# Reordering VectorE and ScalarE work around the block products of a scan and of two attention openings

## The chip, the cores and the metric

The kernel runs on one core of one Trainium2 chip. The metric is the device time of one execution in microseconds (us); lower is better.

## What is computed

Six stages follow each other on one sequence of 256 tokens with 1024 channels, all in float32: convolution mixers, a mixture of 32 experts, stick-breaking attention, a second mixture of experts, a layer with a state-space scan and three groups of dilated attention (called SSD below), and a layer of block attention with 16 heads in two groups of 8 (called MOBA below). Only the last two are touched. Cut to what matters:

```python
# SSD layer; 16 scan heads, then 3 groups of 8 attention heads of 64 channels
proj = rms_norm(x) @ w_in                      # z, x|B|C, dt, q, k, v, gate
xbc  = silu(causal_conv4(xbc)); dt = softplus(dt + dt_bias); a = dt * A
cs   = cumsum(a)                               # one running sum per head
m_h  = (C_g @ B_g.T) * exp(cs_t - cs_s)        # s <= t, per head h
y_h  = m_h @ (x_h * dt_h) + d_skip * x_h
y    = rms_norm(y * silu(z)) * ssd_norm_w
q, k = rope(rms_norm(q)), rope(rms_norm(k))    # per head
o_g  = softmax(q_g @ k_g.T / 8 + mask_g) @ v_g # for each group g of 8 heads
x    = x + concat(y, weighted_sum(o_g) * silu(gate)) @ w_out
# MOBA layer; with 256 tokens there is one block, so it is causal attention
q, k, v, g = split(rms_norm(x) @ w_in)
x = x + (softmax(rope(q) @ rope(k).T / 8 + causal) @ v * silu(g)) @ w_out
```

## The kernel before

**Tiles.** The 256 tokens are two tiles of 128. Weights come as chunks of 2 MB (1024 inputs by 512 outputs) through a ring of slots in SBUF; in the last two stages a ring of three slots is in use and SyncE issues a chunk's load when its slot is free.

**Seven products for a chunk.** A projection to q, k or v of one attention group is one chunk, computed with seven block products in place of eight (a Strassen-like scheme): `seven(g, n)`, n from 0 to 6, each four matmuls of 128x256 (line 1303), which the trace records as x8. Around them stand
- `w_sums(upto)` on VectorE (line 2616): differences of weight quarters, four for a chunk, numbered on through the chunks, "up to" a count; product 1, 2, 4 and 6 each need one more of them;
- `keep(g, n)` on ScalarE (line 1851): three copies of a product's result from PSUM to SBUF. Product 2 writes where product 0's result stood and waits for the first copy, product 3 waits for the second, product 5 for the third;
- `corner(g)` on VectorE (lines 2625 and 2631): additions that build one quarter of the output. Product 6 waits for the first of them;
- `front(g)` and `crossed(g)` on VectorE (lines 2637 and 2644): the remaining additions. `crossed` ends the chunk and frees its PSUM banks for the next chunk's product 0.

**The scan** (SSD) has nine steps n = 0 to 8. In step n TensorE makes two running sums (`run_sum`, line 1496), some of the 21 products of the first group's chunks q, k, v (the list `shares` says how many in each place), the sum of squares of an earlier pair of heads (`square_sums`, line 1522) and the output of the pair before (`y`, lines 1511 and 1514). VectorE makes for two heads `decay` (lines 2813 and 2815, the arguments of the exponentials), `scan` (line 2822, product with C.B), then `gated` (lines 2827 and 2832), and in between the chunk additions, `w_sums` as the table `SCAN_SUMS` says, and `mean_squares` (lines 2572 and 2575) for the norms of q and k. ScalarE makes two exponentials (line 2013), `square` (line 2007), `squared` (line 1861), `head_root` (lines 1871 and 1872) and the copies `keep`.

**An attention group** (`attention`) starts with an opening: 16 transposes of q and k on TensorE (line 696), moved to SBUF by ScalarE (line 1639) and VectorE (line 2103). Four pairs of heads follow, each with scores (lines 1372 and 1373), mask and maximum on VectorE (`masked`, lines 2661 to 2670), exponentials on ScalarE (line 1890), transposes of them (line 1384), moves to SBUF (lines 1900 and 2678), and the product with v (`mix`, lines 1400 and 1403). Between these, TensorE fills in products of the next group's chunks; the list `shares` in `attention` says how many at each place. The groups are numbered 0, 1, 2 (SSD) and 3, 4 (MOBA); `g_no(3)` is group 3. Groups 0, 1 and 3 have a next group whose chunks they project.

**GpSimd** runs `rotate`: from the head norms it scales and rotates q and then k of a group (lines 637 to 661), and the opening of that group waits for both.

Order on each engine is the order in which its part of the code is written; every engine waits for semaphores.

## Time and profile before

| | |
|---|---|
| median of 3 runs | 1681.7 us (1680.41 to 1683.4) |
| the profiled execution's own time | 1688.95 us |
| its span | 1687.0 us |
| TensorE busy | 1574.2 us, 93% of the span |
| VectorE busy | 489.2 us, 29% |
| ScalarE busy | 265.1 us, 16% |
| GpSimd busy | 76.8 us, 5% |
| granted TensorE clock, mean | 0.985 of full |

Busy time says which engine had work recorded, not what set the end. The scan runs from about 1269 to 1333 us of the span, group 0 from 1333 to 1390, group 1 to 1439; group 2 and the output of SSD follow; MOBA's first chunks end at 1571, group 3 from 1571 to 1624, group 4 after it.

### The profile page before, as it was taken

The page shows a single profiled execution, that of the slowest core. Times are in us where ns is not written, and L with a number is a line of the kernel's source. Part 1 is how long each engine was busy: PE and PEld are TensorE (multiplying, and loading weights), DVE is VectorE, ACT ScalarE, POOL GpSimd, SP SyncE. Part 2 cuts the span into 40 slices and gives each one's busy share as a digit, 9 for nine tenths or more (in the row PEclk, how much of TensorE's full clock was granted, in tenths as well). Part 3 has the DMA queues.
Part 4 walks back from the last instruction along what each step waited for, and adds up shares of the span by engine and source line. Part 5 has one row for each costly group of instructions (what it writes and reads, how often), then busy time and mean ns, then how long its engine had stood idle before and what let it go on. Part 6 is the DMA issues. An engine that isn't in the chain of part 4 may idle for free. (4 is left out here: it accounts for less than half of the span.)

```text
span 1687.0 us, 25056 instructions
## 1 busy us (share of the span) xinstructions
PE 1574.2 (93%) x10674; PEld 1045.4 (62%) x10674; DVE 489.2 (29%) x934; ACT 265.1 (16%) x659; POOL 76.8 (5%) x138
## 2 busy tenths in 40 slices
PE   9999999998998899999999989888999989999998
PEld 8855555555455666455555655555887668648774
DVE  4941000000000313520000000004337786356542
ACT  1020000000000112210000000001222323311331
POOL 0000000000000000000000000000000342003020
PEclk9999999999999899999999999998999899999999
DMA  9679999999999832699999999997333123243320
GB/s 388 274 305 385 426 427 429 427 428 428 427 428 426 368 118 106 248 419 409 428 428 427 427 428 428 428 428 298 112 142 145 50 106 145 100 148 113 139 100 25
DMA packets 38520, 502.52 MB, mean 298 GB/s; under 512 B 4273, under 2 KB 4529, under 8 KB 6065
## 3 DMA queue, kind: packets, MB, share of 16 engines
q1 hardware_dynamic: 37872, 499.40, 71.9%
q0 software_dynamic: 576, 2.10, 0.3%
q8 instruction: 53, 0.87, 0.2%
q14 instruction: 19, 0.15, 0.0%
HBM read 500.43 MB, written 1.05 MB: 297 GB/s over the span
## 5 line engine op out<-in xcount | busy, mean ns | idle before, releaser
L854 PE MATMUL ps<-x_tok,tables_sb 128*128 128x256 f32 x1228 | 305.1, 392 | 0.0
L854 PEld LDWEIGHTS ps<-x_tok,tables_sb 128*128 128x128 f32 x1228 | 220.9, 189 | 103.5 <-issue 78.6
L877 PE MATMUL ps<-ring,arena 128*32 128x256 f32 x3968 | 238.6, 382 | 32.5 <-DMA ring<-in_expert_up 23.4
L877 PEld LDWEIGHTS ps<-ring,arena 128*32 128x32 f32 x3968 | 118.7, 109 | 141.3 <-issue 30.7
L719 PE MATMUL ps<-spare,ring 128*128 128x256 f32 x768 | 169.5, 383 | 1.3 <-DVE spare L2108 1.3
L2344 DVE TENSOR_TENSOR arena<-arena,ps 128x128 f32<-128x128 f32 x64 | 18.4, 288 | 499.3 <-ACT arena L1723 499.3
L719 PEld LDWEIGHTS ps<-spare,ring 128*128 128x128 f32 x768 | 147.2, 192 | 22.7 <-DVE spare L2108 1.6
L940 PE MATMUL ps<-ring,arena 128*32 128x512 f32 x928 | 115.1, 612 | 16.3 <-ACT arena L1718 11.3
L1303 PE MATMUL ps<-ring 128*128 128x256 f32 x480 | 114.8, 393 | 3.6 <-issue 3.6
L1303 PEld LDWEIGHTS ps<-ring 128*128 128x128 f32 x480 | 92.8, 196 | 21.9 <-issue 9.2
L751 PE MATMUL ps<-ring,arena 128*128 128x512 f32 x224 | 98.7, 596 | 2.9 <-ACT arena L1841 1.3
L1303 PE MATMUL ps<-ring,spare 128*128 128x256 f32 x360 | 88.6, 397 | 7.7 <-DVE tables_sb L2625 6.0
L1723 ACT ACTIVATE arena<-ps 128x128 f32<-128x128 f32 x64 | 17.8, 278 | 459.1 <-PE ps L877 459.1
L1303 PEld LDWEIGHTS ps<-ring,spare 128*128 128x128 f32 x360 | 69.7, 198 | 21.1 <-DVE ring L2616 6.7
L2616 DVE TENSOR_TENSOR ring<-ring 128x1024 f32<-128x1024 f32 x60 | 73.5, 1259 | 6.0 <-DMA ring<-in_stream 4.8
L751 PEld LDWEIGHTS ps<-ring,arena 128*128 128x128 f32 x224 | 41.7, 190 | 53.8 <-issue 49.1
L899 PE MATMUL ps<-arena,root_w 128*128 128x512 f32 x128 | 59.7, 607 | 14.6 <-DVE arena L2355 13.1
L2355 DVE COPY arena<-ps 128x512 f32<-128x512 f32 x16 | 11.1, 692 | 204.3 <-PE ps L940 204.3
L940 PEld LDWEIGHTS ps<-ring,arena 128*32 128x32 f32 x928 | 26.0, 110 | 69.9 <-issue 67.7
L833 PE MATMUL ps<-arena,x_tok 128*128 128x128 f32 x512 | 60.5, 276 | 0.8 <-DVE arena L2303 0.8
L833 PEld LDWEIGHTS ps<-arena,x_tok 128*128 128x128 f32 x512 | 58.6, 192 | 1.9 <-DVE arena L2303 1.1
L899 PEld LDWEIGHTS ps<-arena,root_w 128*128 128x128 f32 x128 | 22.8, 189 | 52.9 <-DVE arena L2355 27.7
(298 smaller groups left out, 1402.4 us busy)
## 6 DMA issues: line engine op xcount, KB each, us to landing
ring<-in_expert_up SPq DMA_DIRECT2D x124, 2048.0 KB, 20.9
ring<-in_stream SPq DMA_DIRECT2D x43, 2048.0 KB, 8.4
ring<-in_expert_down SPq DMA_DIRECT2D x42, 2048.0 KB, 25.1
ring<-in_expert_down SPq DMA_DIRECT2D x32, 1024.0 KB, 23.3
arena<-in_expert_up SPq DMA_DIRECT2D x4, 2048.0 KB, 11.2
arena<-in_expert_down SPq DMA_DIRECT2D x2, 2048.0 KB, 12.3
tables_sb<-in_expert_down SPq DMA_DIRECT2D x2, 2048.0 KB, 9.9
spare<-in_expert_down SPq DMA_DIRECT2D x2, 2048.0 KB, 10.3
```

Source lines behind the costliest of these rows:

```text
L719: ins = pe.matmul(o, w[:, k, m * P:(m + 1) * P], xT[:, k, :], start=(k == 0), stop=(k == KT - 1))
L751: ins = pe.matmul(bank(2 * t + n), mixT[:, 4 * c + k, t * P:(t + 1) * P], w[:, k, n * 512:(n + 1) * 512], start=(c == 0 and k == 0), stop= ...
L833: ins = pe.matmul(ps[:, b, n * P:(n + 1) * P], x[:, t, k * P:(k + 1) * P], pick[:, t].rearrange("p e s -> p (e s)"), start=(t == 0), stop= ...
L854: pe.matmul(ps[:, b, 0:TOK], ident, x[:, 0, 0:TOK], start=True, stop=True, skip_group_check=True)
L877: ins = pe.matmul(ps[q * SLOTS:(q + 1) * SLOTS, 4 + e % 2, 0:TOK] .rearrange("p (g n) -> p g n", g=2), xg[:, 4 * half + k, e * SLOTS:(e + ...
L899: return pe.matmul(bank(2 * t + n), back[:, t * P:(t + 1) * P], yg[:, n * 512:(n + 1) * 512], start=False, stop=False, skip_group_check=True)
L940: ins = pe.matmul(ps[e * SLOTS:(e + 1) * SLOTS, 6 + n, :], hidT[:, e, k * SLOTS:(k + 1) * SLOTS], v, start=(k == 0), stop=(k == 3), skip_g ...
L1303: ins = pe.matmul(o, i[:, k, :], m[:, k, :], start=(opens and k == 0), stop=(k == 3), skip_group_check=True)
L1723: act.activation(sg[:, e % 2, :], ps[:, 4 + e % 2, 0:P], ACT.Silu).then_inc(s("silu"), 1)
L2344: dve.tensor_tensor(hid[:, e % 2, :], sg[:, e % 2, :], ps[:, 4 + e % 2, P:TOK], mul)\
L2355: dve.tensor_copy(yg[:, 512:], bank(7)).then_inc(s("yg_moved"), 1)
L2616: dve.tensor_tensor(w_sum[n % W_SUMS], a_, b_, sub).then_inc(sem("w_sums"), 1)
```

## The change

Nothing is computed otherwise; instructions change places on three engines. The transposes of group 3's opening go to other PSUM banks (4, 5, 2, 3 in place of 0, 1, 2, 3), since bank 0 takes the next chunk's products.

```diff
-SCAN_SUMS = (10, 12, 12, 15, 16)
+SCAN_SUMS = (10, 12, 12, 14, 15, 15, 16)
...
         def qk_banks(n):
-            return (0, 1, 2, 3) if n == g_no(3) else (4, 5, 2, 3)
+            return 4, 5, 2, 3
...   TensorE, attention
-                shares = [3, 3 if grp != g_no(3) else 4, 3, 4, 3, 4]
+                shares = [3, 3, 3, 4, 3, 4]
...
-                elif parts and grp != g_no(3):
+                elif parts:
                     some(1)
-                elif grp != g_no(3):
+                else:
...   TensorE, scan
-                shares = [2, 2, 3, 2, 2, 3, 2, 1, 1, 1, 1, 1]
+                shares = [2, 2, 3, 2, 2, 3, 1, 1, 2, 1, 1, 1]
...   ScalarE, attention
-                if grp != g_no(3):
-                    keep(q, 1)
+                keep(q, 1)
                 exps(0)
-                if grp == g_no(3):
-                    keep(q, 1)
                 keep(q, 2)
...   ScalarE, scan
                 for n in range(SSD_HEADS // 2):
+                    c = g + 6 + n // 2
+                    if n in (0, 2, 4):
+                        keep(c, 0)
+                    elif n == 5:
+                        keep(c, 1)
                     for h in (2 * n, 2 * n + 1):
                         act.wait_ge(sem("ss_arg"), 2 * (h + 1))
                         act.activation(ss_arg[:, h % 2, :], ss_arg[:, h % 2, :], ACT.Exp)\
                             .then_inc(sem("ss_e"), 1)
-                    c = g + 6 + n // 2
-                    if n in (0, 2, 4):
-                        keep(c, 0)
+                    if n in (0, 2):
                         keep(c, 1)
+                    if n == 5:
+                        keep(c, 2)
                     if n in (2, 4):
                         squared(0, "qk"[(n - 2) // 2])
                     if n >= 1:
                         square(n - 1)
-                    if n in (0, 2, 4):
+                    if n in (0, 2):
                         keep(c, 2)
...   ScalarE, before group 3
                 keep(g + 2, 1)
+                keep(g + 2, 2)
                 head_root(n, "k")
-                keep(g + 2, 2)
...   VectorE, attention (groups 0, 1, 3)
                 masked(3)
-                w_ahead(16)
                 corner(k)
+                w_ahead(14)
                 front(k)
                 crossed(k)
...
                 front(v)
+                w_ahead(15)
                 crossed(v)
+                w_ahead(16)
...   VectorE, scan
-                        if n in (1, 3, 6):
-                            corner(g + 6 + n // 2 - n // 6)
+                        if n in (1, 3):
+                            corner(g + 6 + n // 2)
                         scan(2 * n)
                         scan(2 * n + 1)
-                    if n in (1, 3, 7):
-                        front(g + 6 + n // 2 - n // 7)
                     if n in (1, 3):
+                        front(g + 6 + n // 2)
                         crossed(g + 6 + n // 2)
                     if n >= 1:
                         gated(n - 1)
+                    if n in (3, 5):
+                        mean_squares(0, "qk"[(n - 3) // 2])
                     if n < len(SCAN_SUMS):
                         w_sums(SCAN_SUMS[n])
-                    if n in (3, 5):
-                        mean_squares(0, "qk"[(n - 3) // 2])
+                    if n == 7:
+                        corner(g + 8)
+                        front(g + 8)
                 crossed(g + 8)
...   VectorE, before group 3
                 crossed(g + 1)
-                mean_squares(n, "k")
                 w_sums(c + 14)
                 corner(g + 2)
                 w_sums(c + 16)
                 front(g + 2)
                 crossed(g + 2)
+                mean_squares(n, "k")
```

In groups 1 and 3 the counts of `w_ahead` are capped at what is left of the chunks, and nothing is left for 14, 15 and 16; there `w_ahead` does nothing at the changed places.

How the instructions stand now, at three places. In the changed kernel the same code has line numbers that differ by a few.

VectorE in group 0, at the end of `masked(3)` (last row of it first), before:

```order
L2670 TENSOR_SCALAR spare<-spare 128x2x2
L2616 TENSOR_TENSOR ring<-ring 128x1024 x3
L2625 TENSOR_TENSOR tables_sb<-tables_sb,ps 128x256
L2631 TENSOR_TENSOR arena<-tables_sb 128x256
L2637 TENSOR_TENSOR arena<-tables_sb,ps 128x256
L2644 TENSOR_TENSOR arena<-tables_sb,ps 128x2x256
```

And in the changed kernel (2672 was 2670, 2627 was 2625, 2618 was 2616):

```order
L2672 TENSOR_SCALAR spare<-spare 128x2x2
L2627 TENSOR_TENSOR tables_sb<-tables_sb,ps 128x256
L2633 TENSOR_TENSOR arena<-tables_sb 128x256
L2618 TENSOR_TENSOR ring<-ring 128x1024
L2639 TENSOR_TENSOR arena<-tables_sb,ps 128x256
L2646 TENSOR_TENSOR arena<-tables_sb,ps 128x2x256
```

Three weight differences stood ahead of `corner(k)`; now none does, one stands behind it, and the other two behind `front(v)` and `crossed(v)`.

ScalarE in steps 4 and 5 of the scan (2013 is an exponential, 1851 a copy `keep`, 1861 `squared`, 2007 `square`), before:

```order
L2013 ACTIVATE arena<-arena 128x384 x2
L1851 ACTIVATE tables_sb<-ps 128x256 x2
L1861 ACTIVATE arena<-arena 128x1024
L2007 ACTIVATE arena<-arena 128x256
L1851 ACTIVATE tables_sb<-ps 128x256
L2013 ACTIVATE arena<-arena 128x384 x2
L2007 ACTIVATE arena<-arena 128x256
```

And in the changed kernel (2015 was 2013, 2004 was 2007):

```order
L1851 ACTIVATE tables_sb<-ps 128x256
L2015 ACTIVATE arena<-arena 128x384 x2
L1861 ACTIVATE arena<-arena 128x1024
L2004 ACTIVATE arena<-arena 128x256
L1851 ACTIVATE tables_sb<-ps 128x256
L2015 ACTIVATE arena<-arena 128x384 x2
L1851 ACTIVATE tables_sb<-ps 128x256
L2004 ACTIVATE arena<-arena 128x256
```

The first copy of v's products went ahead of step 4's exponentials, the second to the start of step 5, behind step 4's `square`, the third behind step 5's exponentials.

TensorE in the opening of group 3, from the transposes on, before:

```order
L696 MATMUL ps<-tables_sb,arena 128x128 x16
L1372 MATMUL ps<-arena 128x128
L1373 MATMUL ps<-arena 128x256
L1372 MATMUL ps<-arena 128x128
L1373 MATMUL ps<-arena 128x256
L1303 MATMUL ps<-ring,spare 128x256 x4
L1303 MATMUL ps<-ring 128x256 x8
L1384 MATMUL ps<-tables_sb,spare 128x128 x6
```

And in the changed kernel:

```order
L696 MATMUL ps<-tables_sb,arena 128x128 x16
L1303 MATMUL ps<-ring,spare 128x256 x4
L1372 MATMUL ps<-arena 128x128
L1373 MATMUL ps<-arena 128x256
L1372 MATMUL ps<-arena 128x128
L1373 MATMUL ps<-arena 128x256
L1303 MATMUL ps<-ring 128x256 x12
L1384 MATMUL ps<-tables_sb,spare 128x128 x6
```

Product 0 of the next q chunk now stands between the transposes and the scores that wait for them; one product fewer follows later.

## Rows read from the trace of the kernel before

**Rows 1.** Timeline of TensorE in the scan: start, us, line, [idle before, releaser].

```profile
1272.73 3.69 PE L1303 MATMUL ps<-ring 128*128 128x256 f32 x16 [0.88 <-issue]
...
1307.95 3.75 PE L1303 MATMUL ps<-ring 128*128 128x256 f32 x8 [2.71 <-issue]
...
1326.77 0.70 PE L1522 MATMUL ps<-arena,tables_sb 128*128 128x256 f32 x2 [2.17 <-ACT arena L2007]
...
1329.02 1.12 PE L1511 MATMUL ps<-arena 128*64 128x256 f32 x4 [0.28 <-DVE arena L2822]
...
1335.11 1.09 PE L696 MATMUL ps<-tables_sb,arena 128*128 128x128 f32 x8 [0.61 <-DVEq L2861]
```

**Rows 2.** Timeline of ScalarE in step 4 of the scan.

```profile
1307.48 0.64 ACT L1851 ACTIVATE tables_sb<-ps 128x256 f32<-128x256 f32 x2
```

**Rows 3.** Timeline of VectorE in steps 3 to 7 of the scan.

```profile
1300.70 3.68 DVE L2616 TENSOR_TENSOR ring<-ring 128x1024 f32<-128x1024 f32 x3
...
1305.63 0.48 DVE L2813 SCALAR_TENSOR_TENSOR arena<-ps,tables_sb 128x256 f32<-128x256 f32 x1
...
1309.57 2.06 DVE L2616 TENSOR_TENSOR ring<-ring 128x1024 f32<-128x1024 f32 x1
1312.88 0.48 DVE L2813 SCALAR_TENSOR_TENSOR arena<-ps,tables_sb 128x256 f32<-128x256 f32 x1 [1.26 <-PE ps L1496]
...
1318.29 0.48 DVE L2827 SCALAR_TENSOR_TENSOR arena<-arena,tables_sb,ps 128x256 f32<-128x256 f32 x1 [2.63 <-PE ps L1514]
...
1321.85 0.41 DVE L2625 TENSOR_TENSOR tables_sb<-tables_sb,ps 128x256 f32<-128x256 f32 x1
...
1322.64 2.71 DVE L2822 TENSOR_TENSOR arena<-arena 128x384 f32<-128x384 f32 x2
...
1327.51 1.46 DVE L2822 TENSOR_TENSOR arena<-arena 128x384 f32<-128x384 f32 x2
```

**Rows 4.** Timeline of TensorE in group 0, around its longest idle time.

```profile
1365.08 1.89 PE L1303 MATMUL ps<-ring,spare 128*128 128x256 f32 x8
1372.03 3.65 PE L1303 MATMUL ps<-ring,spare 128*128 128x256 f32 x8 [5.07 <-DVE tables_sb L2625]
```

**Rows 5.** Timeline of VectorE in group 0, after `masked(3)`.

```profile
1367.27 4.28 DVE L2616 TENSOR_TENSOR ring<-ring 128x1024 f32<-128x1024 f32 x3
1371.48 0.41 DVE L2625 TENSOR_TENSOR tables_sb<-tables_sb,ps 128x256 f32<-128x256 f32 x1
```

**Rows 6.** Timeline of TensorE in the opening of group 3.

```profile
1571.46 1.91 PE L696 MATMUL ps<-tables_sb,arena 128*128 128x128 f32 x16
1575.32 0.50 PE L1372 MATMUL ps<-arena 64*128 64x128 f32 x4 [1.95 <-ACT arena L1639]
...
1576.18 3.18 PE L1303 MATMUL ps<-ring,spare 128*128 128x256 f32 x8
1579.16 4.16 PE L1303 MATMUL ps<-ring 128*128 128x256 f32 x16
```

**Rows 7.** Windows of 2 us: PE, PEld, DVE, ACT, POOL busy, granted clock, DMA share.

```profile
1314.00:1316.00 2.00, 2.00 (x7) 1.55 (x6) 1.66 (x4) 0.71 (x2) 1.18 (x2) 0.50 0.00 0
...
1577.00:1579.00 2.00, 2.00 (x6) 1.62 (x5) 1.93 (x5) 0.00 (x0) 0.00 (x0) 0.50 0.62 262
```

**Rows 8.** Timeline of VectorE ahead of group 3.

```profile
1546.40 1.22 DVE L2572 TENSOR_REDUCE spare<-arena 128x16 f32<-128x1024 f32 x1 [1.12 <-ACT arena L1861]
...
1559.42 0.67 DVE L2644 TENSOR_TENSOR arena<-tables_sb,ps 128x512 f32<-128x512 f32 x1
```

**Rows 9.** Timeline of GpSimd ahead of group 3: the rotations of q and of k.

```profile
1537.37 0.22 POOL L637 TENSOR_TENSOR spare<-spare 128x16 f32<-128x16 f32 x1 [102.00 <-ACT spare L1872]
...
1543.87 0.46 POOL L661 TENSOR_TENSOR arena<-arena 128x128 f32<-128x128 f32 x1
...
1558.04 1.43 POOL L661 TENSOR_TENSOR arena<-arena 128x128 f32<-128x128 f32 x1
```

**Rows 10.** Timeline of GpSimd in step 6 of the scan.

```profile
1322.41 2.53 POOL L646 TENSOR_TENSOR arena<-arena,spare 128x512 f32<-128x512 f32 x2
```

## The prediction

> **What bounds the kernel now.** I read the page first: TensorE is busy for nearly all of the span, so an edit can only pay where it waits. Then I read the list of TensorE's waits. Most are in the two mixtures of experts, which the change does not touch. In the scan and the attention groups few are longer than 0.9 us, and I looked at each in the timelines. Three lie where the change works.
>
> In the scan TensorE stands idle four times of note: 0.88, 2.71, 2.17 and 0.28 us, and 0.61 us in the opening behind it [rows 1]. The 2.71 us before 1307.95 are v's product 2. It waits for the first copy of product 0, which ScalarE makes at 1307.48 [rows 2], behind two exponentials. These wait for the decays that VectorE begins only at 1305.63, because three weight differences from 1300.70 (3.68 us) and a reduction stand ahead [rows 3].
>
> In group 0 product 6 of k waits 5.07 us for the first addition of `corner(k)` [rows 4]. That addition took 0.41 us at 1371.48, but from 1367.27 on VectorE was making three weight differences (4.28 us) [rows 5].
>
> In the opening of group 3 the scores wait 1.95 us for ScalarE to move the transposes [rows 6].
>
> After each of these the clock costs again. At 1314 to 1316 and 1577 to 1579 the granted clock is 0.50, the 1.2 GHz level in place of 2.4 [rows 7]. A product takes 1.89 us at full clock and 3.65 or 3.75 us behind the two long waits [rows 1, 4]; behind the 1.95 us it took 3.18 us and the two after it 4.16 us [rows 6]. After idle times of 0.88 us [rows 1] nothing of this is seen: the two products there took 3.69 us together.
>
> **Group 0.** `corner(k)` moves to the end of `masked(3)`, ahead of all three differences. It can start at 1367.27, since product 4 and the copies it waits for are done. So it starts 1371.48 - 1367.27 = 4.2 us earlier, and TensorE waits 5.07 - 4.2 = 0.9 us. Such a wait left the clock alone, so product 6 takes 1.85 and not 3.65 us: 1.8 us more. Together 6.0 us; if the clock falls all the same, 4.2. The three differences now stand one behind `corner(k)` and one each behind `front(v)` and `crossed(v)`. They are needed for products 2, 4 and 6 of the next group's q. The one behind `crossed(v)` (1.23 us, a third of 3.68) is ahead of VectorE's two moves of the next opening; TensorE has 1.8 us of transposes and 1.85 us of a product there, against 0.7 + 1.2 + 1.6 = 3.5 us of VectorE. It fits with nothing to spare: I charge 0.1. **Term: 5.9, bounds 4.1 and 6.0.** In groups 1 and 3 the moved differences are capped away.
>
> **Opening of group 3.** One product (1.83 us from start to start) goes into the wait of 1.95, which the moves and not the transposes set, so the scores start where they did and one product is gone from behind them: 1.8. TensorE then idles 0.1 us, and I expect no fall of the clock: the slow product gives back 3.18 - 1.89 = 1.3, the two after it 4.16 - 3.69 = 0.5. **Term: 3.6, bounds 1.8 and 3.6.** Products 2 and 3 of q need copies, and both come well before the places they now stand at, as in groups 0 and 1, which have this order already and no wait.
>
> What this could cost is `mean_squares` of k, moved from 1546.40 to behind `crossed`, which ends at 1559.42 + 0.67 = 1560.1 [rows 8]. From there: reduction and roots 1.9, and the rotation on GpSimd 1543.87 + 0.46 - 1537.37 = 7.0 us, so 1569.0, against transposes at 1571.46. The other rotation ended at 1558.04 + 1.43 = 1559.5 [rows 9], 13.1 us behind its reduction's start; that length would end at 1573.2, 1.7 us late. But it ran beside four weight differences, and after 1560.1 VectorE has nothing to do there: I take 1569.0 and no cost. The differences that lay beside it should run a little faster and bring `corner` of v earlier: 0.2 us.
>
> **The scan.** Copy 0 ahead of the exponentials takes away the 0.88 us (ScalarE was idle ahead of them). In step 3 two differences stand in place of three (-1.23). So the decays of step 4 start at 1305.63 - 0.88 - 1.23 = 1303.5, 2.1 us earlier.
>
> From there VectorE is what bounds. Before, it went from 1305.63 to the end of the last scans, 1327.51 + 1.46 = 1328.97: 23.3 us, of which 1.26 + 2.63 = 3.9 were idle, both waiting for TensorE while it ran at half clock. In step 6 `corner(v)` (1322.64 - 1321.85 = 0.8) goes behind the last scans. One difference comes in addition (1.23 us free, 2.06 as the one at 1309.57 took). So 23.3 - 3.9 - 0.8 + 1.2 or 2.1 = 19.8 or 20.7 us, and the last scans end at 1323.3 or 1324.2: 5.7 or 4.8 us earlier. `corner(v)` behind `gated(6)` (0.9 + 0.4) is covered by the last `y`, which took 1.1 us and more from 1329.02.
>
> Against this stand new waits. v's product 3 now needs copy 1, which is behind `square(3)`: decays 1.3, scans 1.2 to 2.7, `gated` 0.9 to 1.5, square 0.4, copy 0.4 from 1303.5 on, so 1307.7 to 1309.8, and TensorE is there at about 1307 (1307.95 - 2.71 - 0.88 = 1304.4, a running sum that waits for the decays, and product 2): a wait of 0.7 to 2.8 where 2.71 was. At its long end the clock falls as before, and the 3.9 us of VectorE's idle time come back. The wait of 2.17 us for `square(5)` stays, since step 6's scans meet the rotation of k again (2.71 us at 1322.64 against 1.46 at 1327.51, beside the GpSimd rows at 1322.41 [rows 10]). The difference now in step 6 makes a second wait of some 2 us ahead of the last `y`, and then v's product 6 may run at half clock (+1.8). The gain lies between 0.6 (5.7 less 3.9 and less 1.2 for locked scans) and 5.7; nearer the free end, since the lighter step 3 acts in any case. **Term: 4.3, bounds 0.6 and 5.7.**
>
> Here a rule speaks against the change. The two scans at 1322.64 took 2.71 us while GpSimd multiplied [rows 10]. The Trainium skill, page "SBUF — State Buffer", on the engine ports, says that VectorE's second port pair is shared with GpSimd as an exclusive lock: an instruction with two SBUF inputs and a GpSimd instruction do not share, one waits for the other to end. The trace agrees with it. By it the rotation of q, which now starts earlier, would catch the scans of step 4 (2.7 us, not 1.2) and the difference behind them (2.06, not 1.23), and the term would be 4.3 - 1.5 - 0.8 = 2.0, the sum 11.7.
>
> **Sum.** 5.9 + 3.6 + 0.2 + 4.3 = 14.0 us. The profiled execution took 1688.95 us (span 1687.0 and 1.95 around it), 7.25 more than the median of 1681.7; 1688.95 - 14.0 = 1674.95, and at the median's level 1681.7 - 14.0 = **1667.7 us**.
>
> **The rivals.**
> - *All three waits go (forecast), 0.60*: 1667.7; its own bounds 1681.7 - 15.5 = 1666.2 and 1681.7 - 9.9 = 1671.8 (with 2.5 or less of the scan, 4.1 in group 0).
> - *The scan gives nothing, 0.18*: product 3 waits 2.8 us in place of product 2, the clock falls, and VectorE's idle time returns. 5.9 + 3.6 + 0.2 + 0.6 = 10.3, so 1671.4. For it: the copy is behind `square(3)`, which is behind locked scans. Against it: TensorE has one product more to do before it needs the copy.
> - *Group 0's wait moves on, 0.08*: with a later weight difference the next group's q waits for one of its sums, or the 0.9 us are enough for the clock. It takes back 4: 1671.7 to 1673. Against it: product 4 of q is some 7 us behind the opening.
> - *Group 3's opening waits for the rotation, 0.05*: 1.7 us late, then the clock falls as behind 1.95 us; the term of 3.6 is gone: 1671.3.
> - *The change doesn't do what it says, 0.05*: each wait has a second cause just behind the first that no row of before shows. 1681.7, give or take 1.5.
> - *Slower, 0.04*: the clock. What spares the time must not bring it down elsewhere. In the scan it was still at 0.50 in the window from 1314 to 1316 [rows 7], 6 to 8 us behind the wait that ended at 1307.95. Half clock costs a half of its length, so against 14.0 us gained it decides from 28 us of new half clock on, and 35 us make 1685. Place: the scan's last three steps, with two waits of 2 us close together, and on into group 0. Against it: behind the waits of 2.17 and 0.28 us the eight transposes at 1335.11 took 1.09 us [rows 1], at the rate of the sixteen in 1.91 [rows 6].
>
> **How the numbers follow.** What a measurement of this kernel can tell from no change is about 0.2%, 3.4 us. Faster by more (below 1678.3): 0.60 + 0.18 + 0.08 + 0.05 = 0.91, less 0.02 for mixtures of the bad cases, 0.89. Same: 0.05 + 0.02 = 0.07. Slower: 0.04. The range reaches from the best bound less the runs' own spread of 1.5 us, 1664.5, to the worse cases with the low bounds of two terms at once, 1681.7 - 6 = 1675.7.
>
> **What would show it.** Group 0: product 6 of k begins within 1 us of product 5's end and takes 1.9 us. Group 3: a product stands between transposes and scores, idle time ahead of the scores under 0.3 us, the clock at 1.00 behind it, and the transposes not held by GpSimd. Scan: v's product 2 without a wait, one ahead of product 3 of 0.7 to 2.8 us, two of about 2 us in steps 7 and 8. The forecast is wrong if the clock is at 0.50 for over 10 us of the scan, if a wait of 1 us or more stands in group 1's start, or if the transposes of group 3 wait for the rotation.

## The result and the profile after

The changed kernel takes **1670.7 us** in the median of 4 executions (1668.54 to 1672.73), against 1682.0 (1680.41 to 1683.4) beside it. The ratio is 0.9919, interval 0.9903 to 0.9936: 13.6 us less, 10.8 to 16.3. The two medians stand 11.3 us apart, which the interval holds too. The forecast was 1667.7 us with 14.0 us gained. On a second chip the ratio was 0.991 (0.9891 to 0.9929). Single executions far above the rest, at a low granted clock, are left out of every ratio, and so is the trace of the first series of the scan's part below, which is of one (2698.5 us at 0.555).

The first lines of the page of the changed kernel:

```profile
span 1669.8 us, 25056 instructions
...
PE 1565.3 (94%) x10674; PEld 1039.7 (62%) x10674; DVE 487.1 (29%) x934; ACT 264.9 (16%) x659; POOL 73.1 (4%) x138
```

The same instructions on the same engines; TensorE is busy for 8.9 us less (the span is 17.2 shorter). The same matmuls took less time, at a mean granted clock of 0.990 for 0.985.

**Three stretches.** I measure each from one TensorE row to another. *Scan*: from the start of q's product 1 in step 1 (before: the 8 matmuls that end where the wait of 0.88 us begins, 2.77 us ahead of the row of 1272.73 [rows 1]; after: the row of 24 at 1268.53, since no wait divides them) to the second half of group 0's transposes. *Group 0*: from there to group 1's transposes. *Opening 3*: from group 3's transposes to the next ones. The rows at the ends that are not shown elsewhere, of before:

```profile
1269.96 1.89 PE L1303 MATMUL ps<-ring 128*128 128x256 f32 x8
...
1390.22 1.91 PE L696 MATMUL ps<-tables_sb,arena 128*128 128x128 f32 x16
...
1623.89 1.91 PE L696 MATMUL ps<-tables_sb,arena 128*128 128x128 f32 x16
```

and of the change:

```profile
1377.94 1.91 PE L696 MATMUL ps<-tables_sb,arena 128*128 128x128 f32 x16
...
1606.62 1.91 PE L696 MATMUL ps<-tables_sb,arena 128*128 128x128 f32 x16
```

| stretch | before | after | gained | forecast |
|---|---|---|---|---|
| scan | 65.15 | 60.21 | 4.9 | 4.3 |
| group 0 | 55.11 | 49.20 | 5.9 | 5.9 |
| opening 3, with group 3 | 52.43 | 49.00 | 3.4 | 3.6 |

The three add up to 14.3 us. The span is 17.2 shorter: 1.4 us of the rest lie ahead of the scan, and 1.6 us at the first chunks of MOBA, in a place that the change does not touch (see "A fourth place" below).

TensorE in the scan after the change, timeline:

```profile
1268.53 5.34 PE L1303 MATMUL ps<-ring 128*128 128x256 f32 x24
...
1303.93 1.99 PE L1303 MATMUL ps<-ring 128*128 128x256 f32 x8
1307.25 1.97 PE L1303 MATMUL ps<-ring 128*128 128x256 f32 x8 [1.33 <-ACT tables_sb L1851]
...
1316.99 0.70 PE L1522 MATMUL ps<-arena,tables_sb 128*128 128x256 f32 x2 [0.16 <-ACT arena L2004]
...
1321.19 0.65 PE L1511 MATMUL ps<-arena 128*64 128x256 f32 x4 [2.70 <-DVE arena L2826]
...
1322.74 3.65 PE L1303 MATMUL ps<-ring,spare 128*128 128x256 f32 x8 [0.68 <-DVE tables_sb L2627]
...
1328.74 1.09 PE L696 MATMUL ps<-tables_sb,arena 128*128 128x128 f32 x8 [0.61 <-DVEq L2867]
```

The waits of 0.88 and 2.71 us [rows 1] are gone: v's product 2 is the row of 1303.93, without idle time. Product 3 has one of 1.33 for its copy. The 2.17 us for `square(5)` have become 0.16. A new wait of 2.70 us stands ahead of the last `y`, where 0.28 was, and behind it v's product 6 takes 3.65 us. The same stretch in windows of 2 us (PE, PEld, DVE, ACT and POOL busy, then the granted clock, the DMA share and GB/s):

```profile
1322.00:1324.00 2.00, 1.32 (x5) 1.11 (x4) 1.86 (x6) 0.42 (x1) 0.58 (x1) 0.70 0.00 0
1324.00:1326.00 2.00, 2.00 (x6) 1.55 (x6) 0.31 (x1) 0.42 (x1) 0.00 (x0) 0.50 0.03 8
```

The clock of 0.50 is the level of 1.2 GHz.

VectorE in steps 3 to 8 of the same scan; L2618 is the weight difference, L2826 the two scans of a step:

```profile
1299.39 2.55 DVE L2618 TENSOR_TENSOR ring<-ring 128x1024 f32<-128x1024 f32 x2
...
1303.19 2.28 DVE L2826 TENSOR_TENSOR arena<-arena 128x384 f32<-128x384 f32 x2
...
1306.30 1.48 DVE L2618 TENSOR_TENSOR ring<-ring 128x1024 f32<-128x1024 f32 x1
...
1314.10 1.21 DVE L2826 TENSOR_TENSOR arena<-arena 128x384 f32<-128x384 f32 x2
...
1316.41 2.06 DVE L2618 TENSOR_TENSOR ring<-ring 128x1024 f32<-128x1024 f32 x1
...
1319.71 1.42 DVE L2826 TENSOR_TENSOR arena<-arena 128x384 f32<-128x384 f32 x2
```

and GpSimd beside them:

```profile
1302.69 2.36 POOL L646 TENSOR_TENSOR arena<-arena,spare 128x512 f32<-128x512 f32 x2
...
1314.81 2.58 POOL L646 TENSOR_TENSOR arena<-arena,spare 128x512 f32<-128x512 f32 x2
```

Two differences stand where three stood, and the decays follow at 1301.86. The scans of step 4 ran into the rotation of q (2.28 us), those of step 6 began ahead of the multiplications of k's (1.21), and the difference behind them ran into it (2.06).

TensorE in group 0 and in the opening of group 3, the answers to [rows 4] and [rows 6]:

```profile
1361.45 1.97 PE L1303 MATMUL ps<-ring,spare 128*128 128x256 f32 x8 [0.85 <-DVE tables_sb L2627]
...
1557.62 1.91 PE L696 MATMUL ps<-tables_sb,arena 128*128 128x128 f32 x16
1559.36 1.89 PE L1303 MATMUL ps<-ring,spare 128*128 128x256 f32 x8
1561.47 0.50 PE L1372 MATMUL ps<-arena 64*128 64x128 f32 x4 [0.21 <-ACT arena L1639]
...
1562.33 5.45 PE L1303 MATMUL ps<-ring 128*128 128x256 f32 x24
```

Product 6 of k waits 0.85 us in place of 5.07 and runs at full clock. In group 3 a product stands between transposes and scores, and the 24 matmuls behind are at full clock.

### The profile page after: what moved, and what is told of

Its sections match the earlier page's. It is cut to its first block and busy times, and to the rows that moved or that the text cites. A ratio compares the mean times of both kernels' runs of the same rounds, so it can differ in the third digit from the quotient of the medians.

```text
span 1669.8 us, 25056 instructions
## 1 busy us (share of the span) xinstructions
PE 1565.3 (94%) x10674; PEld 1039.7 (62%) x10674; DVE 487.1 (29%) x934; ACT 264.9 (16%) x659; POOL 73.1 (4%) x138
## 5 line engine op out<-in xcount | busy, mean ns | idle before, releaser
L940 PE MATMUL ps<-ring,arena 128*32 128x512 f32 x928 | 114.2, 608 | 16.9 <-ACT arena L1718 11.3
L1303 PE MATMUL ps<-ring 128*128 128x256 f32 x480 | 110.4, 383 | 1.3 <-ACT tables_sb L1851 1.3
L2618 DVE TENSOR_TENSOR ring<-ring 128x1024 f32<-128x1024 f32 x60 | 72.8, 1243 | 8.9 <-DMA ring<-in_stream 7.6
```

The source lines that it names most:

```text
L940: ins = pe.matmul(ps[e * SLOTS:(e + 1) * SLOTS, 6 + n, :], hidT[:, e, k * SLOTS:(k + 1) * SLOTS], v, start=(k == 0), stop=(k == 3), skip_g ...
L1303: ins = pe.matmul(o, i[:, k, :], m[:, k, :], start=(opens and k == 0), stop=(k == 3), skip_group_check=True)
L2618: dve.tensor_tensor(w_sum[n % W_SUMS], a_, b_, sub).then_inc(sem("w_sums"), 1)
```

## The experiments

Every kernel was timed between executions of the kernel before on the same chip. The table gives them all; "less" is the time below before by the ratio, with its interval, and the three stretches are those of its trace, measured as above.

| kernel | executions | median us | ratio (95%) | us less | scan | group 0 | opening 3 |
|---|---|---|---|---|---|---|---|
| before, again | 12 | 1684.36 | 1.0007 (0.9994, 1.002) | -1.2 | 65.18 | 55.09 | 52.44 |
| group part alone | 6 | 1675.77 | 0.9951 (0.9936, 0.9966) | 8.2 | 62.12 | 49.21 | 50.74 |
| the same, again | 12 | 1677.46 | 0.9949 (0.9931, 0.9966) | 8.6 | 65.18 | 49.21 | 50.75 |
| opening alone | 12 | 1680.97 | 0.9977 (0.9966, 0.9989) | 3.9 | 65.18 | 55.08 | 49.02 |
| scan alone | 12 | 1680.75 | 0.9979 (0.9965, 0.9993) | 3.5 | none | none | none |
| the same, again | 12 | 1681.91 | 0.9988 (0.9976, 1.0001) | 2.0 | 60.23 | 55.77 | 52.38 |
| the change, again | 6 | 1669.96 | 0.991 (0.9891, 0.9929) | 15.2 | 60.19 | 49.21 | 49.01 |
| difference out of the scan | 5 | 1668.29 | 0.9909 (0.989, 0.9928) | 15.3 | 56.62 | 50.11 | 49.02 |
| ... and the others shifted | 6 | 1667.79 | 0.9902 (0.9883, 0.9922) | 16.5 | 56.61 | 49.22 | 49.01 |
| change without rotation | 6 | 1666.77 | 0.9905 (0.9882, 0.9929) | 16.0 | 55.91 | 49.21 | 49.01 |
| corner alone | 11 | 1681.98 | 0.999 (0.9977, 1.0003) | 1.7 | 66.92 | 53.36 | 52.43 |
| dummies in the opening | 12 | 1682.92 | 1.0 (0.9984, 1.0016) | 0.0 | 61.29 | 55.10 | 50.75 |

**Before, once more.**

> The kernel before, unchanged, profiled once more. Theory A (the traces of before and of the change show what a usual execution does): the same three waits of 2.7, 5.1 and 1.9 us, each followed by half clock, and a span near 1687 us. Theory B (the profiled execution of before lost more to the clock than a usual one): the waits are the same, but the stretch at half clock behind the 2.7 us wait is absent or much shorter than the 9 us seen, and the span is near 1680. Timed: within 0.1% of before.

The trace repeats that of before to 0.03 us in all three stretches, so theory B fell for the trace. Its executions spread from 1679.4 to 1690.3 us; a reason showed itself only in the later traces, below.

**The change, once more.**

> The change as it is, once more, on the chip of the other kernels of this call, so that they can be set against it and not only against the kernel before. If the gain of the change is steady from chip to chip the ratio to before is 0.992 again (0.9903 to 0.9936). Its trace should again have the wait of 2.7 us ahead of the last y of the scan and product 6 of v at half clock (3.6 us) behind it; if that wait was an accident of one execution it is gone.

Both hold: ratio 0.991, a wait of 2.69 us ahead of the last `y`, product 6 of v in 3.34 us behind it, and all three stretches within 0.02 us of the first trace.

**One part at a time.** The group's part is the moved calls in `attention`:

```diff
-                w_ahead(16)
                 corner(k)
+                w_ahead(14)
                 front(k)
...
                 front(v)
+                w_ahead(15)
                 crossed(v)
+                w_ahead(16)
```

> The kernel before with only the attention groups' part on VectorE: corner(k) ahead of the weight differences, one difference behind it, one each behind front(v) and crossed(v). Both theories: the 5.07 us wait of group 0 falls to 0.9 us and product 6 of k takes 1.9 us. Theory A: 5.9 us faster (1676). Theory B: also 5.9 if the clock falls behind 5 us in every execution, 4.2 if it doesn't.

The opening's part is the banks, the product between transposes and scores, the copy ahead of the exponentials, the third copy of v ahead of `head_root`, and `mean_squares` of k behind `crossed`:

> The kernel before with only the third opening's part (banks, shares, one product between transposes and scores, copy 1 ahead of the exponentials, mean_squares of k behind crossed). Theory A: 3.4 us faster. Theory B: 1.8 us for the product that is gone, and up to 1.8 more as far as the clock falls behind the 1.95 us wait in a usual execution. A rotation that holds the transposes would show as a wait of TensorE in front of line 696.

The scan's part is the rest of the diff:

> The kernel before with only the scan's part on all three engines. Theory A: 4.9 us faster, as between the two traces. Theory B: the half clock of 9 us was particular to the profiled execution of before; without it VectorE's 3.9 us of idle time are not there to be won, and the part is worth about 2 us.

The opening's gain is 3.4 us in its stretch and 3.9 in the time. The group's part loses 5.9 us in group 0, as expected, and 8.2 in the time: more than its own stretch. Its trace shows where. In the opening of group 3, which it does not touch, the wait of 1.95 us is still there, and the product behind it takes 1.99 us and not 3.18 [rows 6]:

```profile
1565.23 0.50 PE L1372 MATMUL ps<-arena 64*128 64x128 f32 x4 [1.95 <-ACT arena L1639]
1565.55 0.61 PE L1373 MATMUL ps<-arena 64*128 64x256 f32 x4
1566.09 1.99 PE L1303 MATMUL ps<-ring,spare 128*128 128x256 f32 x8
1567.92 3.62 PE L1303 MATMUL ps<-ring 128*128 128x256 f32 x16
```

So I ran it again:

> The group's part alone again: its first time was 8.3 us below that of before by the means, 2.4 more than the 5.9 that its group 0 lost in the trace, and in its trace the scan, which nothing touched, was 62.1 us long for 65.2, since the half clock behind the wait of 2.71 us was shorter, and the opening of group 3 was 50.7 for 52.4, since it had none at all. Theory A (those falls of the clock come and go from execution to execution, whatever group 0 does): the trace may have them again, with the scan at 65.2, 62.1 or 61.3 us, group 0 is 49.2 us in any case, and the time is nearer to 5.9 less than before: ratio 0.9955 to 0.9970. Theory B (a shorter wait in group 0 keeps falls away elsewhere, so that the part is worth more than its local 5.9): the scan and the opening are short again, and the ratio is 0.995 or less.

Group 0 is 49.21 us again and the opening 50.75, at full clock, with its wait of 1.95 in place; the time is 8.6 us less. The scan, however, is 65.18 this time. So the answer is split. In the opening the traces speak for B, but there are only six: before, before again, the scan alone and the corner alone (below) have the fall (52.4), the two of the group's part do not. Chance is not excluded. 5.9 + 1.7 = 7.6 us of the 8.2 and 8.6 are accounted for, and the fourth place (below) has 1.4 and 1.7 more. In the scan it is A.

The scan's part alone was run twice for its trace:

> The scan's part alone again, for its trace. Theory A (each local gain of the change's trace is the part's own): scan from the first product of q to the second transposes 60.2 us against 65.1 of before, and 4.9 us off the time, ratio 0.997. Theory B (the executions that were profiled exaggerate, and what the scan gains is given back behind it): the scan is 60.2 us in the trace too, but a stretch behind it, as group 0, is longer by what is missing, and the time is 2 to 3.5 us less, ratio 0.998 to 0.999.

Its scan is 60.23 us, the change's own. Group 0 is 0.7 us longer than before (55.77): the half clock behind the wait of 5.05 us lasted on into the output products. That leaves 4.9 - 0.7 = 4.2 us in these stretches, and 1.7 us more at the fourth place, against 3.5 and 2.0 measured, the second with an interval from below nothing to 4.0. In size the times are those of theory B, but of what is given back the trace shows only the 0.7.

**A fourth place.** Behind the transposes that open MOBA, TensorE waits 1.69 or 1.70 us in every one of the thirteen traces, for VectorE (L2108 in the kernel before). No kernel here changes anything there. Before:

```profile
1518.42 3.44 PE L1303 MATMUL ps<-ring,spare 128*128 128x256 f32 x8 [1.69 <-DVE spare L2108]
```

and the change:

```profile
1506.15 1.99 PE L1303 MATMUL ps<-ring,spare 128*128 128x256 f32 x8 [1.69 <-DVE spare L2110]
```

The product takes 3.36 to 3.44 us in the traces of before, before again, opening alone, corner alone and dummies, and 1.99 in the eight that have the group's or the scan's part. So 1.4 to 1.7 us of the gain of every such kernel are full clock in code that nothing touched. Five traces against eight, with no exception, are hard to put down to chance. But the reason is open: the scan's part alone keeps group 0's wait of 5.05 us, so a shorter wait in group 0, as theory B has it, is not what all eight share.

**The scan of before differs from execution to execution.** Seven traces, of kernels that differ only behind it, have the scan of before: 65.15, 65.18, 62.12, 65.18, 65.18, 66.92 and 61.29 us. The wait of 2.71 us is in all of them, and ends in the same matmul. In the kernel with dummies, whose scan is that of before:

```profile
1307.18 1.96 PE L1303 MATMUL ps<-ring 128*128 128x256 f32 x8 [2.71 <-issue]
...
1309.71 1.99 PE L1303 MATMUL ps<-ring 128*128 128x256 f32 x8
```

In the group's part alone, first time:

```profile
1308.23 3.46 PE L1303 MATMUL ps<-ring 128*128 128x256 f32 x8 [2.71 <-issue]
...
1312.25 1.99 PE L1303 MATMUL ps<-ring 128*128 128x256 f32 x8
```

In before, once more:

```profile
1309.28 3.75 PE L1303 MATMUL ps<-ring 128*128 128x256 f32 x8 [2.71 <-issue]
1312.97 1.22 PE L1496 MATMUL ps<-arena,tables_sb 16*128 16x256 f32 x4
1314.12 3.78 PE L1303 MATMUL ps<-ring 128*128 128x256 f32 x8
```

The same wait is followed by no half clock (one trace), by one product of it (one), or by two products and what lies between (five). And in the kernel with the corner alone product 6 of v falls too:

```profile
1330.03 3.78 PE L1303 MATMUL ps<-ring,spare 128*128 128x256 f32 x8
```

which took 2.26 us in before. The mean of the seven is 64.4, so the changed scan, 60.2 in all its three traces, gains 4.2 us in the mean, and anything from 1.1 to 6.7 against one of them.

**The corner alone.** Kernel before, with the corner ahead of the differences, but the differences in one piece:

```diff
-                w_ahead(16)
                 corner(k)
+                w_ahead(16)
                 front(k)
```

> Kernel before, with the corner of k in group 0 ahead of the differences, but all three differences of the group directly behind that corner and none behind the others, so that the order is right for product 7 and no difference is spread out. Theory A (only the corner of k was late; what is behind it has slack): the wait of 5.07 us is gone and the group is 5.9 us shorter, as with the change. Theory B (spreading counts as well: three differences of 1.23 to 1.43 us ahead of the front of k make product 0 of v or its corner wait): 2 to 4 us of waits come behind product 7 and the gain is 2 to 4 us.

TensorE in group 0:

```profile
1369.06 1.97 PE L1303 MATMUL ps<-ring,spare 128*128 128x256 f32 x8 [0.85 <-DVE tables_sb L2625]
...
1374.84 3.63 PE L1303 MATMUL ps<-ring,spare 128*128 128x256 f32 x8 [2.20 <-DVE arena L2644]
```

and VectorE:

```profile
1369.59 4.26 DVE L2616 TENSOR_TENSOR ring<-ring 128x1024 f32<-128x1024 f32 x3
1373.77 0.41 DVE L2637 TENSOR_TENSOR arena<-tables_sb,ps 128x256 f32<-128x256 f32 x1
1374.10 0.68 DVE L2644 TENSOR_TENSOR arena<-tables_sb,ps 128x512 f32<-128x512 f32 x1
```

The wait of 5.07 us is 0.85, exactly as with the change, and a new one of 2.20 stands ahead of v's product 0, for `crossed(k)`, which now comes behind 4.26 us of differences. The clock falls behind that one (3.63 us for 1.89). The group gains 1.75 us in place of 5.9, a little under the 2 to 4 of theory B; in kind B holds. Moving the addition takes the wait away; spreading the three differences is what keeps it away.

**The difference in step 6.** The changed kernel with the sixteenth difference left to group 0:

```diff
-SCAN_SUMS = (10, 12, 12, 14, 15, 15, 16)
+SCAN_SUMS = (10, 12, 12, 14, 15)
```

> The change with one weight difference less in the scan: the sixteenth, which in the changed kernel stood in step 6 between the last mean square of k and the last decays (2.06 us on VectorE), is made in group 0 behind the fifteenth. Theory A (that difference makes the decays late): the wait of 2.70 us ahead of the last y falls to under 1.3 us, product 6 of v runs at full clock (1.9 for 3.6 us), and 2.5 to 3.5 us are gained on the change; the fifth difference in group 0 lies ahead of the copy of v's last piece and costs nothing there, since product 7 has 8 matmuls of cover. Theory B (the decays wait for ScalarE's exponentials or for the mean square itself, not for the difference): the wait stays above 2 us and the time is that of the change within 0.5 us. Theory C (the difference is as dear in group 0): the scan gains 2 to 3 and group 0's wait of 0.85 us grows by as much as one difference, 1.2 us: 1 to 1.5 us net.

TensorE:

```profile
1315.81 0.65 PE L1511 MATMUL ps<-arena 128*64 128x256 f32 x4 [0.90 <-DVE arena L2826]
...
1317.24 1.97 PE L1303 MATMUL ps<-ring,spare 128*128 128x256 f32 x8 [0.56 <-DVE tables_sb L2627]
...
1336.44 1.97 PE L1303 MATMUL ps<-ring,spare 128*128 128x256 f32 x8 [0.66 <-DVE tables_sb L2627]
```

Theory A holds for the scan: 2.70 fell to 0.90, product 6 of v runs at full clock, 3.6 us gained. Theory C holds in part: with five differences in one piece ahead of the copy of P, the transposed exponentials (5.96 us for 4.83), the corner of q is late by 0.66 us and group 0 is 0.9 us longer. Net 2.7 us in the trace; the time, 15.3 us less where the change has 15.2 beside it, does not show it.

The last step shifts every difference of group 0 to the next place and puts one into VectorE's idle time behind the last move of o:

```diff
-                w_ahead(8)
+                w_ahead(8 - late)
...                 the same for 10, 13 and 14; late = grp == 0
                 move_o(1)
+                w_ahead(14)
                 corner(v)
```

> As the kernel with the sixteenth difference out of the scan, but each place of group 0 makes the difference that the next one made: four in front, then two, three and one, and one that is new behind the last move of o and ahead of the corner of v, where VectorE is idle for 1.25 us. Theory A (a fifth difference in front made the copy of P and the corner of q late, which is the wait of 0.66 us there): that wait is gone, group 0 is 49.2 us again for 50.1, the trace is 0.9 us shorter than with the fifth in front and 3.5 us shorter than the change; ratio to before near 0.989 to 0.990. Theory B (the place in front costs nothing, the wait has another cause): group 0 stays at 50.1 us. Theory C (the new place is as dear: the corner of v comes late and group 1's opening waits): group 0 or group 1's transposes wait up to 1.2 us.

Theory A: group 0 is 49.22 us, the scan still 56.61. VectorE at the new place:

```profile
1370.21 0.69 DVE L2685 COPY arena<-ps 128x512 f32<-128x512 f32 x1 [0.16 <-DVE arena L2884]
1370.82 1.46 DVE L2618 TENSOR_TENSOR ring<-ring 128x1024 f32<-128x1024 f32 x1
1372.20 0.41 DVE L2627 TENSOR_TENSOR tables_sb<-tables_sb,ps 128x256 f32<-128x256 f32 x1
```

Its stretches are 3.6 us shorter than the change's. The time is 1667.8 us in the median, ratio 0.9902, where the change had 0.9919 and 0.991: in the right direction, but the intervals overlap. It beats the kernel before for certain and the change by the trace only.

**GpSimd beside VectorE.** The changed kernel without the rotation of group 0's q and k, which attends over unrotated queries and keys:

```diff
+                    if grp == 0 and SSD in on:
+                        pool.sem_inc(sem("at_qk"), 1)
+                        continue
```

> The change without the rotation of q and k of group 0 on GpSimd (the multiplications and additions there are left out, so that group 0 attends over keys and queries that are not rotated; the semaphore still counts). Theory A (GpSimd's two-source operations are what lengthens VectorE's in the scan): the pairs of scans of 2.28 and the first one's 2.55 us fall to 1.2 to 1.5 us, the difference of 2.06 in step 6 to 1.2 to 1.4, the wait of 2.70 ahead of the last y falls below 1.9 us, and the scan is 1 to 3 us shorter: ratio to before 0.990 to 0.991. Theory B (VectorE's own traffic or ScalarE's is what lengthens them): they stay as they are and the time is that of the change.

VectorE (three lines further down in this file: L2829 for L2826, L2621 for L2618):

```profile
1299.60 1.21 DVE L2829 TENSOR_TENSOR arena<-arena 128x384 f32<-128x384 f32 x2
...
1301.65 1.22 DVE L2621 TENSOR_TENSOR ring<-ring 128x1024 f32<-128x1024 f32 x1
...
1311.47 1.22 DVE L2621 TENSOR_TENSOR ring<-ring 128x1024 f32<-128x1024 f32 x1
```

Theory A, and stronger than I priced it. 2.28 fell to 1.21, 1.48 and 2.06 to 1.22. (The first two differences took 2.55 us in both kernels: they never met the rotation, and my expectation was wrong to name them.) The wait ahead of the last `y` is 1.63, product 6 of v is at full clock, and the scan is 55.91, 4.3 us less than the change's: some 1.7 of it is product 6 at full clock (3.65 - 1.97), and the wait of product 3, 1.33, is 0.26. This too is from the traces: the time, 16.0 us less, stands within the interval of the change's.

**Dummies in the opening.**

```diff
+                if parts and grp == g_no(3):
+                    pe.wait_ge(sem("at_proj"), projected[0])
+                    keep_warm(4)
                 wait_T(qk_turn(grp))
```

> Kernel before with four dummy matmuls (128x128 by 128x256, into a bank that nothing reads) in the opening of group 3, behind the transposes, in the place where TensorE is idle for 1.95 us until the rotation of q is done; they are not reference work. Nothing else moves. Theory A (the granted clock fell there because TensorE was idle, and the product and the scores behind it ran at half speed for that reason): the fall is gone or comes later, the 8 matmuls behind take 1.9 us for 3.18 and those behind them are short too, and the opening gains 1.3 to 1.8 us: ratio 0.999. Theory B (the clock falls whatever stands there, by what the engine did before): half clock stays, opening unchanged or up to 0.5 us longer.

TensorE waits there for ScalarE's moves of the transposes [rows 6]; the expectation names the rotation, which is wrong. In the trace the dummies are 8 matmuls in 1.89 us, the wait is 0.22, the product behind takes 1.99 us, and the opening is 1.7 us shorter, as theory A says. But the group's part alone had the same 50.75 us with the wait of 1.95 and no dummies. So the run does not tell the theories apart, and the time, 0.0 us less with an interval of 2.7 on either side, doesn't either. Inconclusive.

## Why the prediction was right

**Group 0, 5.9 forecast, 5.9 in the trace.** The corner's start, the 0.9 us that are left (0.85) and full clock behind them came as worked out. The 0.1 us charged for the difference behind `crossed(v)` was not paid: from group 1's transposes to its scores it is 3.57 us in both traces. In the time the part alone is worth more, 8.2 to 8.6 us; in its two traces the falls in the opening of group 3 and at the fourth place were missing as well.

**Opening of group 3, 3.6 forecast, 3.4 in the trace.** The product in the wait, the full clock behind, and the rotation that is in time were right. The rotation ended at 1554.2, 3.4 us ahead of the transposes, where I had 2.5. The 0.2 us for differences that meet no rotation did not come: before product 6 of v TensorE waits 1.03 us for 0.94, since the differences there wait for a load. In the traces with the group's part the half clock of this opening is gone anyway, so the two parts overlap and that piece of 1.7 counts once. The parts alone add up to 8.2 + 3.5 + 3.9 = 15.6 us, against 13.6 and 15.2 for the whole; their intervals are too wide to show the overlap in the time.

**The scan, 4.3 forecast, 4.9 in the trace, 4.2 against the mean of seven, 2.0 and 3.5 by itself in the time.** Of its steps: copy 0 (0.88) right; step 4's decays at 1303.5 right (1301.86, and the changed scan starts 1.43 earlier, so 1303.3); the wait of product 3 (0.7 to 2.8 forecast) 1.33, right; the new wait of about 2 us ahead of the last `y` 2.70, and product 6 of v at half clock, right. Wrong was that the 2.17 us for `square(5)` would stay, because step 6's scans would meet the rotation of k. They ran ahead of it in 1.21 us, and 0.16 us were left. The rotation met the difference behind them instead (2.06 us), and the last wait was 2.70 where I had 2. So the last scans ended at 1321.1, 6.4 us earlier on that count, where 4.8 or 5.7 were forecast. Wrong too was that the last `y` covers `corner(v)`: product 6 waits 0.68 us for it. And product 6's half clock was charged against full clock (+1.8), but before it already took 2.26 us, at half clock in part behind the wait of 2.17, which the forecast did not price; it lost 1.4. From the last `y` to the second transposes the change takes 7.55 us for 6.09: 6.4 - 1.5 = 4.9. The 4.3 itself was a choice between 0.6 and 5.7 and not a sum of these steps, so that it came within 0.6 is in part luck.

**The rule on the ports** (the Trainium skill, page "SBUF — State Buffer", section "Who interferes with whom") struck where I had said it would: 2.28 us in step 4. The run without rotation shows that GpSimd is the cause, in 2.28 against 1.21 us. Its own sum, 11.7 us, was too low in this trace: it priced the scans of step 4 at 2.7 us and the difference behind them at 2.06, and they took 2.28 and 1.48. But it is inside the interval of the result, 10.8 to 16.3, so the time alone does not decide between it and 14.0.

**The level.** I took the 14.0 us from the median of before. The traces say how executions of one kernel can be 7 us apart: the same scan costs 61.3 to 66.9 us, by the clock. Ahead of the scan, in code that is the same in all thirteen traces, they differ by 6.4 us (q's product 1 starts at 1264.94 to 1271.30), and there too half clock lasts longer in some: from 560 to over 572 us of the span in before, and to 564 with the difference out of the scan. How much of the 7.25 this is, is not shown, since executions that are not profiled have no trace. The forecast was 3.0 us below the median measured. That 14.0 is so near 13.6 is luck in part: the medians alone give 11.3, the second chip 15.2, and the traces hold 1.6 us at the fourth place that the forecast did not have. In the range two small slips stand, 1666.2 - 1.5 is 1664.7 and not 1664.5, and the 9.9 us take 2.0 us of the scan and not 2.5; neither changes the outcome.

**The rivals.** The scan that gives nothing: no. Group 0's wait that moves on: not in the changed kernel, but it is just what the corner alone shows, 2.20 us and half clock for v's product 0. So the rival was real and was kept out by the spreading, whose part in the term I had not named; my price for it, 4 us, is about what it cost (5.9 - 1.75 = 4.2). Opening 3 behind the rotation: no. Slower by the clock: no. From the scan's start to the end of group 3 half clock follows five waits of before (2.71, 2.17, 5.07, 1.69 and 1.95 us) and one of the change (2.70).

## What to carry to other kernels

When an instruction that somebody waits for stands behind a block of work that nobody waits for yet, moving it ahead is half of the edit; the block then stands ahead of the next instruction that somebody waits for. Split the block into single pieces and give each an idle place: here that was worth 4.2 of 5.9 us, and one such piece in the wrong place (step 6) cost 3.6 us, both by the traces. Before you price a stall from one trace, look at a second execution of the same kernel for the clock behind it: the wait repeated to 0.01 us, its half clock did not.

## What the runs showed of the hardware

- The same idle time of TensorE is not always followed by a lower clock. Behind 2.71 us of it the half clock lasted for two products (3.75 and 3.78 us), for one (3.46) or for none (1.96), in seven traces of the same scan. The scan was 61.3 to 66.9 us long by that.
- Behind 1.95 us in the opening of group 3 it fell in all four traces with group 0 as it was or with a wait of 2.20 in it (product of 3.10 to 3.42 us behind, stretches of 52.4), and in neither of the two where group 0 had lost its long waits (1.99). Why a place 200 us behind should notice is open. Behind 1.69 us in the opening of MOBA it fell in five traces (3.36 to 3.44 us) and in none of the eight with the group's or the scan's part (1.99).
- Behind waits of 0.85, 0.88, 0.90 and 1.33 us, with no longer one close ahead of them, the products ran at full clock (1.85 to 1.97 us each).
- Two scans of 128x384 on VectorE took 1.21 us without GpSimd at work and 2.28 beside its multiplications (x1.9); a difference of 128x1024 1.22 and up to 2.06.
